# Where the root of the norms enters: an unnormalised x turned by column halves, in a kernel of eight sublayers on one Trainium2 core

## The reference, cut to what matters

```python
def rms_norm(x, w):
    y = x * lax.rsqrt(jnp.mean(x * x, axis=-1, keepdims=True) + EPS)
    return y * w
# sublayer 0: x = x + 0.5 * swiglu(rms_norm(x), ...)      ffn0
#          1: x = x + mamba2_mixer(rms_norm(x), ...)      SSM
#          2: x = x + 0.5 * swiglu(...)                   ffn1
#          3: x = x + 0.5 * swiglu(...)                   ffn2
#          4: x = x + mla_mixer(...)                      MLA
#          5: x = x + 0.5 * swiglu(...)                   ffn3
#          6: x = x + rmsnorm(three mixers of rmsnorm(x)) b2
#          7: x = x + rmsnorm(swiglu(rmsnorm(x)))         ffn4
def swiglu(h, w_gate, w_up, w_down):
    return (silu(h @ w_gate) * (h @ w_up)) @ w_down
```

## Time and profile before

| | us |
|---|---|
| median of 3 runs | 1866.71 |
| lowest and highest | 1863.03, 1867.37 |
| the profiled execution | 1867.34 |
| its span | 1865.6 |
| TensorE busy | 1778.4 (95%) |
| VectorE busy | 1181.3 (63%) |
| ScalarE busy | 856.7 (46%) |
| POOL busy | 80.3 (4%) |
| mean granted TensorE clock | 0.974 of full |

### The profile page before, as it was taken

The page is one execution under the profiler, slowest core; times in us unless marked ns, Lnnn a source line. Parts: engine busy times, 40 slices in busy tenths (PEclk is TensorE's granted clock), DMA queues, the critical chain, the costliest instruction groups (busy, mean ns, idle before and its releaser), DMA issues.

```text
span 1865.6 us, 24850 instructions
## 1 busy us (share of the span) xinstructions
PE 1778.4 (95%) x9667; PEld 1532.9 (82%) x9667; DVE 1181.3 (63%) x1305; ACT 856.7 (46%) x1033; POOL 80.3 (4%) x130
## 2 busy tenths in 40 slices
PE   8999999989999999999789999999998799989998
PEld 7888899877888888887678888987886687878887
DVE  5666797645766666666756666765557473566665
ACT  5444657644434443435434343654335434444433
POOL 0000001310000000001000000001000000000000
PEclk9999999989999999999699999999999899999999
DMA  7655464324555555644224555463552264445552
GB/s 235 199 181 182 148 191 137 113 87 139 189 194 185 174 179 182 194 152 147 68 68 150 188 190 176 147 203 130 186 181 91 91 203 156 160 140 186 194 188 90
DMA packets 212801, 298.28 MB, mean 160 GB/s; under 512 B 12341, under 2 KB 168570, under 8 KB 212730
## 3 DMA queue, kind: packets, MB, share of 16 engines
q1 hardware_dynamic: 212730, 297.30, 48.8%
HBM read 296.21 MB, written 1.05 MB: 159 GB/s over the span
## 4 chain that ended last, share of the span: by engine, by line
PE 88%; DVE 5%; ACT 4%; issue 2%; POOL 1%; DMA 0%; POOLq 0%; DVEq 0%; ACTq 0%
PE PS L383 25%; PE PS L389 13%; PE PS L316 12%; PE PS L317 11%; PE PS L318 11%; PE PS L374 2%; PE PS L376 2%; PE PS L375 2%; PE PS L655 2%; ACT whi L300 1%; DVE wlo L305 1%; PE PS L824 1%; DVE x_sb L586 1%; ACT xn L597 0%; PE PS L1191 0%
## 5 line engine op out<-in xcount | busy, mean ns | idle before, releaser
L305 DVE TENSOR_TENSOR wlo<-raw,whi 128x2048 fp32r<-128x2048 f32 (+1 forms) x284 | 642.3, 2264 | 227.5 <-ACT whi L300 226.9
L300 ACT ACTIVATE whi<-raw 128x2048 fp32r<-128x2048 f32 (+1 forms) x284 | 536.3, 1890 | 453.1 <-PE PS L389 334.6
L383 PE MATMUL PS<-XT,whi 128*128 128x512 f32 x2016 | 504.5, 393 | 2.2 <-DVE XT L639 2.2
L383 PEld LDWEIGHTS PS<-XT,whi 128*128 128x128 f32 x2016 | 366.9, 189 | 70.7 <-issue 2.6
L389 PEld LDWEIGHTS PS<-XT,wlo 128*128 128x128 f32 x2016 | 274.4, 190 | 19.2
L389 PE MATMUL PS<-XT,wlo 128*128 128x256 f32 x2016 | 280.3, 282 | 0.0
L316 PE MATMUL PS<-whi,aTh 128*128 128x512 f32 x400 | 156.2, 391 | 0.0
L317 PE MATMUL PS<-wlo,aTh 128*128 128x512 f32 x400 | 156.2, 391 | 0.0
L318 PE MATMUL PS<-whi,aTl 128*128 128x512 f32 x400 | 155.6, 389 | 0.0
L316 PE MATMUL PS<-whi,XT 128*128 128x512 f32 (+2 forms) x384 | 152.6, 397 | 1.3 <-ACT V L1723 1.1
L318 PE MATMUL PS<-whi,XT 128*128 128x512 f32 (+2 forms) x384 | 148.5, 387 | 0.0
(11 more groups left out here) (356 smaller groups left out, 2229.1 us busy)
## 6 DMA issues: line engine op xcount, KB each, us to landing
raw<-in_w_in SPq DMA_DIRECT2D x112, 512.0 KB, 4.5
raw<-in_ffn_w_gate SPq DMA_DIRECT2D x88, 512.0 KB, 4.5
raw<-in_ffn_w_up SPq DMA_DIRECT2D x88, 512.0 KB, 4.4
raw<-in_ffn_w_down SPq DMA_DIRECT2D x88, 512.0 KB, 4.1
raw<-in_ssm_w_in SPq DMA_DIRECT2D x48, 512.0 KB, 4.5
raw<-in_w_ffn_in SPq DMA_DIRECT2D x44, 512.0 KB, 4.2
raw<-in_w_ffn_out SPq DMA_DIRECT2D x22, 512.0 KB, 4.1
raw<-in_ssm_w_out SPq DMA_DIRECT2D x16, 512.0 KB, 4.0
```

The costliest lines, as they stand in the source:

```text
L300: act.activation(whi[s][:, 0:size], raw[s][:, 0:size], ACT.Copy).then_inc(hi_done, 1)
L305: dve.tensor_tensor(wlo[s][:, 0:size], raw[s][:, 0:size], whi[s][:, 0:size].bitcast(FP32), ALU.subtract).then_inc(lo_done, 1)
L383: return pe.matmul(o, whi[n % SLOTS][:, sl], XT[:, k, :, :].rearrange("p a n -> p (a n)"), start=(k == 0), stop=False)
```

## The change

x is turned as it is, without the root. The last product of a sublayer is done in four quarters (`last_product`); x is added in four quarters of 128x512, in the order in which the left columns of both tiles come first (`BY_HALF`), or tile by tile where b2 and ffn4 end (`BY_TILE`). Eight plain transposes of the left half of x (`turn_x`, part 0) stand in TensorE's program before the fourth quarter (behind the whole product before sublayer 7), the eight of the right half inside the first product of the next sublayer. In a feed-forward sublayer the root comes in as a factor on the summed gate, one VectorE multiply of 128x512 a round, by a row of roots that one float32 product spreads over the partitions (`spread_rstd`, `row_act`); for the up half it is a factor where the down product is added to x (`rstd_half`). `mul_first_pairs` now takes the first gate and up blocks together. In the SSM mixer and b2 a block of columns that needs no turned root goes first (z, 512 columns; mv, 512 columns), with the root as a scale where it is copied out; in the meantime a second, scaled copy of the turned x is made for all that follows (`scaled_dve`, `scaled_act`). In MLA the root is a scale in the squares and where cq and ckv are copied out, and one small multiply for the rotary key. The SSM mixer's `z_block`s that remain are six, and their order shifts by two. `mul_rows` and `mul_out` do all that needs the high part of a weight block first. In `post_dve` the root has a tile of its own, and for ffn4 one more small multiply. SP waits for quarters of x, and stores the output in four pieces.

The diff, cut to its core; what it leaves out are the waits and names that follow from this, the scale arguments in MLA and b2's copies, and the splits' positions in ScalarE's and VectorE's programs (one block of the next sublayer instead of two is made low before the norm; row_act, the copy of block bc0 or mqk0, scaled_act and the copy of z or mv follow each other on ScalarE):

```diff
@@ -178,12 +178,13 @@
...
+        N["z"] = natural_blocks(win, 0, 1)
         N["bc0"] = feature_blocks(win, 2 * D_INNER, 1)
...
         N["xs"] = feature_blocks(win, D_INNER, 8)
-        N["z"] = natural_blocks(win, 0, 4)
+        N["z_rest"] = natural_blocks(win, 512, 3) - 2
...
@@ -198,11 +199,12 @@
...
         ffn_add(3)
+        N["mv"] = natural_blocks(in2, C_MV, 1)
...
         N["mqk"] = feature_blocks(in2, C_MQ + 2 * P, 7) - 1
-        N["mv"] = natural_blocks(in2, C_MV, 2)
...
@@ -317,19 +333,29 @@
...
+        def by_high(pe, o, lh, ll, rh, start):
+
+            pe.matmul(o, lh, rh, start=start, stop=False)
+            pe.matmul(o, ll, rh, start=False, stop=False)
+
...
-            wait_block(pe, n, it)
+            wait_high(pe, n, it)
             for k in part:
                 if ready is not None:
                     pe.wait_ge(*ready(k0 + k))
                 sl = slice(k * width, (k + 1) * width)
                 for t in range(NT):
                     ts_ = slice(t * P, (t + 1) * P)
-                    m = mm3(pe, banks[t], Xh[:, k0 + k, ts_], Xl[:, k0 + k, ts_], whi[s][:, sl], wlo[s][:, sl],
-                            first and k == 0, last and k == nk - 1)
+                    by_high(pe, banks[t], Xh[:, k0 + k, ts_], Xl[:, k0 + k, ts_], whi[s][:, sl], first and k == 0)
+            wait_block(pe, n, it)
+            for k in part:
+                sl = slice(k * width, (k + 1) * width)
+                for t in range(NT):
+                    m = pe.matmul(banks[t], Xh[:, k0 + k, t * P:(t + 1) * P], wlo[s][:, sl], start=False,
+                                  stop=last and k == nk - 1)
             if part[-1] == nk - 1:
...
@@ -342,26 +368,54 @@
...
+        def last_product(pe, n, lefts, order, norm=None):
+
+
+
+            wait_block(pe, n)
+            for q, (t, c) in enumerate(order):
+                if q == 3 and norm is not None:
+                    turn_x(pe, norm, 0)
+                for k in range(2):
+                    m = mul_out_part(pe, n, lefts, t, k, False, True, halves=(c,))
+                m.then_inc(*((quarter_done, 1) if q < 3 else (block_used, 1)))
+
+        def mul_first_rows(pe, n, norm, banks, width, Xh, Xl, spread):
+
+
+
+            mul_rows(pe, n, 0, 0, 4, width, banks, True, False, Xh, Xl, lambda k: normed(norm, k), range(3))
+            turn_x(pe, norm, 1)
+            mul_rows(pe, n, 0, 0, 4, width, banks, True, False, Xh, Xl, lambda k: normed(norm, k), range(3, 4))
+            if spread is not None:
+                spread_rstd(pe, norm, spread)
+            mul_rows(pe, n + 1, 0, 4, 4, width, banks, False, True, Xh, Xl, lambda k: normed(norm, k))
 
         def mul_features(pe, n, bank, it=0):
...
@@ -400,31 +454,62 @@
                     m = low_by_high(pe, banks[:, c, :], n, c, k)
             m.then_inc(block_used, 1)
 
-        def mul_first_pairs(pe, n, norm, banks):
-
+        def mul_first_pairs(pe, n, norm, gate, up):
...
+            first, second = range(KD // 2), range(KD // 2, KD)
+            wait_high(pe, n)
+            for k in first:
+                pe.wait_ge(*normed(norm, k))
+                for c in range(2):
+                    high_by_both(pe, gate[:, c, :], n, c, k)
+            turn_x(pe, norm, 1)
+            wait_block(pe, n)
+            for c in range(2):
+                for k in first:
+                    low_by_high(pe, gate[:, c, :], n, c, k)
+            wait_high(pe, n + 1)
+            if norm:
+                pe.wait_ge(*added(norm, 3))
+            for c in range(2):
+                for k in first:
+                    high_by_both(pe, up[:, c, :], n + 1, c, k)
+            for k in second:
+                pe.wait_ge(*normed(norm, k))
+                for c in range(2):
+                    high_by_both(pe, gate[:, c, :], n, c, k)
+            for c in range(2):
+                for k in second:
+                    m = low_by_high(pe, gate[:, c, :], n, c, k)
+            m.then_inc(block_used, 1)
+            spread_rstd(pe, norm, PS[:, 0, 0:SEQ])
+            for c in range(2):
+                for k in second:
+                    high_by_both(pe, up[:, c, :], n + 1, c, k)
+            wait_block(pe, n + 1)
+            for c in range(2):
+                for k in range(KD):
+                    m = low_by_high(pe, up[:, c, :], n + 1, c, k)
+            m.then_inc(block_used, 1)
...
@@ -458,15 +543,14 @@
...
+        def ffn_pe(pe, i, norm, after):
             n0, f0 = N[f"ffn{i}"], NFF * i
-            mul_first_pairs(pe, n0, norm, GATE0)
-            mul_pairs(pe, n0 + 1, UP)
+            mul_first_pairs(pe, n0, norm, UP, UP0)
 
             mul_pairs(pe, n0 + 2, GATE)
...
 
             hi_upto(act, at, n0 + 2)
+            row_act(act, norm, PS[:, 0, 0:SEQ])
...
@@ -519,14 +604,17 @@
 
                 dve.wait_ge(block_used, ready)
                 dve.tensor_reduce(out=ff_s[:, :, :], in_=halves_of(gate), axis=AX.X, op=ALU.add)\
+                   .then_inc(F["gate_added"], 1)
+                dve.wait_ge(F["gate_added"], f0 + j + 1)
+                dve.tensor_tensor(ff_s[:, :, :], ff_s[:, :, :], rstd_row.unsqueeze(1).to_broadcast([P, 2, SEQ]), ALU.mult)\
                    .then_inc(F["gate_summed"], 1)
...
@@ -569,93 +658,136 @@
...
+        def turn_x(pe, i, c):
+
+
+            if i:
+                pe.wait_ge(*added(i, (1 if c == 0 else 3) if i < 7 else 2 + c))
+            else:
+                for t in range(NT):
+                    pe.wait_ge(x_in[t], 16)
+            for k in range(c * KD // 2, (c + 1) * KD // 2):
+                for t in range(NT):
+                    m = pe.transpose(x_turned(k)[:, t * P:(t + 1) * P], xs_[:, t, k * P:(k + 1) * P], ident[:, :])
+                if k % 2:
+                    m.then_inc(S_N["t_done"], 1)
+
+        def spread_rstd(pe, i, o):
+
+            pe.wait_ge(S_N["diag_done"], NT * ROWS_OF_RSTD[i])
+            pe.matmul(o, ones[:, 0:P], diag, start=True, stop=True).then_inc(S_N["spread_done"], 1)
+
+        def row_act(act, i, o):
+            act.wait_ge(S_N["spread_done"], ROWS_OF_RSTD[i])
+            act.activation(rstd_row, o, ACT.Copy).then_inc(S_N["row_done"], 1)
+
+        def adds(dve, i, order, used, scale):
+
+            def add(q):
+                t, c = order[q]
+                dve.wait_ge(*((quarter_done, 3 * (i - 1) + q + 1) if q < 3 else (block_used, used)))
+                dve.scalar_tensor_tensor(out=xs_[:, t, c * 512:(c + 1) * 512], in0=psD[:, 2 * t + c, :], scalar=scale(t),
+                                         in1=xs_[:, t, c * 512:(c + 1) * 512], op0=ALU.mult, op1=ALU.add)\
+                   .then_inc(x_added, 1)
             return add
...
+        def norm_act(act, i, col, Xh=XTh):
             S = S_N
+
+            def high(c):
+                for k in range(c * KD // 2, (c + 1) * KD // 2):
+                    act.wait_ge(S["t_done"], 4 * i + k // 2 + 1)
+                    act.activation(Xh[:, k, :], x_turned(k), ACT.Copy, scale=cols[0][:, col + k:col + k + 1])\
+                       .then_inc(S["h_done"], 1)
+
+            high(0)
             for t in range(NT):
                 if i == 0:
...
-                act.wait_ge(S["t_done"], 4 * i + c // 2 + 1)
-                act.activation(XTh[:, c, :], x_turned(c), ACT.Copy,
-                               scale=cols[0][:, col + c:col + c + 1]).then_inc(S["h_done"], 1)
-
-        def norm_act(act, i, col):
...
+        def variance(dve, i):
+            dve.wait_ge(S_N["sq_done"], NT * (i + 1))
+            dve.tensor_scalar(var[:, :], stat[:, :], 1.0 / DM, EPS, ALU.mult, ALU.add).then_inc(S_N["var_done"], 1)
+
+        def rstd_tables(dve, i):
+
+            dve.wait_ge(S_N["rstd_done"], i + 1)
+            dve.tensor_scalar(rstd_half[:, :], rstd[:, :], 0.5, None, ALU.mult).then_inc(S_N["half_done"], 1)
+            if i in ROWS_OF_RSTD:
+                for t in range(NT):
+                    dve.tensor_scalar(diag[:, t * P:(t + 1) * P], ident[:, :], rstd[:, t:t + 1], None, ALU.mult)\
+                       .then_inc(S_N["diag_done"], 1)
+
+        def x_low(dve, i, col, c, Xh=XTh, Xl=XTl):
...
+        def norm_dve(dve, i, col, add, at=None, upto=None, Xh=XTh, Xl=XTl):
+
+
+            if i:
+                for q in range(3):
+                    add(q)
+            x_low(dve, i, col, 0, Xh, Xl)
+            if i:
+                add(3)
+            if upto is not None:
+                lo_upto(dve, at, upto)
+            variance(dve, i)
+            if upto is not None:
+                rstd_tables(dve, i)
+            x_low(dve, i, col, 1, Xh, Xl)
+            if upto is None:
+                rstd_tables(dve, i)
...
+        def scaled_dve(dve, i, col):
+
+
+            s0 = KD if i == 6 else 0
+            dve.wait_ge(S_N["row_done"], ROWS_OF_RSTD[i])
+            for c in range(2):
+                ks = range(c * KD // 2, (c + 1) * KD // 2)
+                for k in ks:
```

(30 more changed lines are left out.)

415 lines of the change are left out of this document (207 added, 208 removed).

## The result

| | before | after |
|---|---|---|
| median of 4 runs each, us | 1864.87 | 1849.62 |
| lowest and highest | 1862.44, 1867.37 | 1848.78, 1853.19 |
| ratio after / before | | 0.9928, 95% interval 0.9914 to 0.9941 |
| the profiled execution | 1867.34 | 1849.32 |
| its span | 1865.6 | 1847.6 |

The changed kernel is 0.7% faster. The forecast was 1850. Two of its terms were off, though, by nearly five and by four us with opposite signs, and this document is mostly about them.

A forecast was written before the change was run, and what follows sets the result against it. TensorE, 88% of the chain of waits, was taken as the bound, its time lost at norm stops. Norms 28.9 less 12 for SSM groups gave 16.9; 1867.34 - 16.9 - 0.6 = 1850 us, range 1839 to 1861.

The forecast's parts named there:

- Norms of sublayers 2, 3, 5 and 6: Gaps of TensorE ahead of these sublayers: no wait of weight left, winning 5.9, 5.9, 6.3 and 3.3 us.
- the second rival: Clock lost at the norms' turns (12 us over seven norms), or SSM groups slow throughout: 1862 us; chance 0.14.
- Sublayers 0 and 1, head: Start and SSM head: -2.0 us (between 0 and -3) and +1.6 us (between -1 and 3.8).
- The wait ahead of i=2: SSM head: TensorE waits on the first convolution's first tap, behind the late third feature block load; 1.7 us.
- Term -12: SSM groups 4 and 5 left bare: two stops, 6.9 us, plus 2.5 of clock each; between -7 and -18.
- The cheap case: Rival: the bare SSM groups cost their stops alone, 7 us, giving 1845, down to 1838; chance 0.14.
- MLA, 4.1: Norm ahead of the MLA mixer (sublayer 4): 6.36 less 1.8 of TensorE work and 0.4 of wait, 4.1 us won.
- High parts first: Row products doing high weight parts first: saves a fraction of a us, left at 0.
- I had subtracted 0.6: Step from the profiled execution of before, 1867.34, to the median, 1866.71: 0.6 us taken off the forecast.
- Sublayer 7 and the end, 3.8: Last feed-forward norm: 12.24 less 8.9 gives 3.3 us, between 1 and 5.5; program end with earlier quarters, 0.5.
- The gate factor, 0: Feed-forward rounds: 55 VectorE multiplies of 0.692, 38 us in all, costed at nothing because covered.
- my 1.46: VectorE's wait ahead of each of 55 sums of up, 1.46 us, claimed to cover the 0.69 gate factor.

The follow-up runs named there:

- Experiment 3: Changed kernel with 14 products of 512 columns that nobody reads behind the outputs of SSM groups 4, 5 and 6: 1842.92 us, ratio 0.9898 to before.
- experiment 6: Changed kernel with row and output products back in the old order (high, low weights, low x in turn, behind the low split): 1855.46 us, ratio 0.9961 to before.
- Experiment 5: Changed kernel with the gate factor multiplied three times a round, extra results unread: 1852.59 us, ratio 0.9948 to before; five times: 1862.21 us, ratio 0.9997.

## Why the prediction was right, and where it was not

**Norms of sublayers 2, 3, 5 and 6.** Right to 0.2 us each: the count of quarters, adds and copies gave no wait, and there was none. The eight turns took 1.03 to 1.04 with their drain, and each spread 0.59. The first half of the second rival (clock lost at the turns) is out. The Trainium skill, TensorE: Matmul & The Clock Gate, Part 4 on the PE-mode transpose, says that transposes do not engage the full clock. These traces neither bear that out nor contradict it: the turns of sublayers 1 to 6 had products on both sides, and none let the clock fall. At sublayer 7 it did fall, behind a stop of 2.99 and eight turns (the eight products behind them were granted 0.56 and took 3.39); what part the turns had in that is not shown.

**Sublayers 0 and 1, head.** Right. The SSM head without its half blocks of z went from 105.9 to 103.4 between the product and the first scores: 2.5 won, or 1.6 with the first turns (0.9) that stand ahead of that cut, as forecast; the second trace of the changed kernel has 1.6 less. The wait ahead of i=2 was 2.0 for a forecast 1.7.

**"Two more stops of 3.46 are 6.9 ... 2.5 for each of the two groups. Term -12".** This is the step that failed. The stops were 3.54 and 3.40, as said. The clock was not: I let it come back within a group, as dense products had brought it back behind a norm. With a stop of 3.4 in each round and narrow products between, it never came back: scores, outputs, scores and the tail each lost 2.3 to 2.6, 9.5 in all, for the 5 that I took. The measured term is -16.6, near the bad end of the range that I gave it (-18). The cheap case is out; the second half of the second rival, groups slow throughout, is what happened behind the first bare stop. Experiment 3 shows that it was the standing still: the same products with the stops filled kept their speed.

**MLA, 4.1.** Measured 8.3, in three parts that add up to it within 0.2: 4.3 for the norm (the projection's products end 5.2 earlier in the sublayer, and 0.9 of that are turns counted elsewhere), 0.9 from a wait on low weights that is gone, and 3.3 from the profiled execution of before, whose heads got their clock back late. The last of these is no term of the change at all. The 0.9 is the term "High parts first", which I had left at 0: with TensorE's old order (experiment 6) 0.68 of waits on low weights stand there again. The MLA sublayer of that trace is no longer for it, though, so it is not shown that the 0.9 reaches the time. As for the 3.3, I had subtracted 0.6 for how that execution stood to the median of three; against the medians of the later comparisons, 1862.4 to 1863.0, it stood nearly 5 high.

**Sublayer 7 and the end, 3.8.** Measured 4.7: the post-norm let the turn start 3.0 behind the product, not 4.2, and the half clock cost 1.4 instead of 1.0.

**The gate factor, 0.** The price was right, the cover was another than I had named: the factor went into the 0.72 that VectorE stood ahead of the low split, and in the steady rounds the wait ahead of the sum of up, my 1.46, stayed as it was. Experiment 5 shows that this wait would have covered it too.

So the forecast of 1850 for a result of 1849.6 rests on two errors that cancelled: -4.6 in the groups, +4.2 in MLA, of which 3.3 were the profiled execution of before. That it came out to within 1 us was luck. Against the median of before in the experiments the change wins 12.6 us (1862.4 to 1849.8), where the terms had 16.9; the groups' 4.6 are about the difference. Either error alone would have left the time inside the range. Of the rest no term was off by over 1 us.

## What to carry to other kernels

Filler (independent work that stands between two dependent steps) is worth what it covers plus the clock behind it. Before moving it out of a stage, price the bare stage at the lower clock throughout, not just its stops. When there are fewer fillers than gaps, cut them smaller; here a stop of 0.6 to 0.8 kept the full clock and one of 3.5 took it. Where nothing is left to fill with, products that nobody reads can stand in as long as they end before the wait does: here 14 in each of three gaps gave 7 us of 1850 back. And a forecast built on one profiled execution inherits what that execution lost by chance: trace the kernel before twice.

## What was not expected of the hardware

- The clock's return differs between executions of one kernel: MLA heads by 3.3 us (before, two traces). Between traces of nearly the same kernels sixteen products at the start took 3.92 or 5.52 us, and a stop of 1.90 was harmless in one and worth 4 us in another.
- Behind float32 products of ones, read by nobody, the first real products ran at full speed (eight in 2.16 us instead of 3.75): a pass of ones took 0.45 us at first and 0.25 later. The granted clock in the profile reads 1.00 over all of it, so at the start of the program it is the durations that tell.
- Scores and outputs, mostly products of 64 to 256 columns, ran at the full clock to the end with the stops filled (1.23 for ten outputs), and without did not regain it over 29 us, from 383.4 to 412, with two stops of 3.3 to 3.4 among them.
